# Differential attention: ScalarE copies turned weights ahead of the exponentials in every batch, the second rotary swap moves behind the first output, and unit 7's coefficients are made one batch sooner

## The reference

```python
q1, q2 = _rope(qb[:, :, 0], cos, sin), _rope(qb[:, :, 1], cos, sin)
k1, k2 = _rope(kb[:, :, 0], cos, sin), _rope(kb[:, :, 1], cos, sin)
p1 = jax.nn.softmax(jnp.where(mask, z1, -jnp.inf), axis=-1)     # z1 = q1 k1^T * scale, block of 128 queries
p2 = jax.nn.softmax(jnp.where(mask, z2, -jnp.inf), axis=-1)
w = p1 - lam * p2
out = w @ v
```

## Time and profile before

| what | value |
|---|---|
| median of 3 runs | 1461.81 us |
| profiled execution | 1462.43 us |
| its span | 1460.6 us |
| TensorE matmul busy | 1441.8 us (99%) |
| VectorE busy | 1010.9 us (69%) |
| ScalarE busy | 675.2 us (46%) |
| GpSimd busy | 356.9 us (24%) |
| granted TensorE clock | 0.998 of full |

### The profile page before, as it was taken

How to read it: one execution, slowest core, us unless ns; L and a number is a source line. 1 busy time by engine, 2 the same in 40 slices (tenths; PEclk the granted TensorE clock), 3 DMA queues, 4 the chain that set the end, 5 groups by cost and what they waited for, 6 DMA issues and landing times. The chain is left out here.

```text
span 1460.6 us, 19172 instructions
## 1 busy us (share of the span) xinstructions
PE 1441.8 (99%) x6960; PEld 1198.1 (82%) x6960; DVE 1010.9 (69%) x1293; ACT 675.2 (46%) x1092; POOL 356.9 (24%) x278
## 2 busy tenths in 40 slices
PE   9999999999999999999999999999999999999997
PEld 7888888887888888888888878888888888888886
DVE  6676876778868668574456788666664567678767
ACT  4454554546557667442122335444444434433343
POOL 4544454456444244212330220000000000000004
PEclk9999999999999999999999999999999999999999
DMA  5111112111111001013632334444444588836553
GB/s 198 44 39 49 58 44 72 57 58 59 44 46 42 30 15 43 30 58 101 211 106 83 114 99 163 179 146 144 154 158 154 206 276 295 293 131 200 190 198 132
DMA packets 76832, 172.38 MB, mean 118 GB/s; under 512 B 6097, under 2 KB 30929, under 8 KB 76625
## 3 DMA queue, kind: packets, MB, share of 16 engines
q1 hardware_dynamic: 76752, 171.33, 34.4%
HBM read 127.27 MB, written 44.04 MB: 117 GB/s over the span
## 5 line engine op out<-in xcount | busy, mean ns | idle before, releaser
L783 PE MATMUL p_proj<-xt_h,w_hi 128*128 128x512 f32 x616 | 244.3, 397 | 0.0
L787 PE MATMUL p_proj<-xt_h,w_lo 128*128 128x512 f32 x616 | 243.2, 395 | 0.0
L785 PE MATMUL p_proj<-xt_l,w_hi 128*128 128x512 f32 x616 | 241.7, 392 | 0.0
L2329 POOL TENSOR_TENSOR w_lo<-w_raw,w_hi 128x512 fp32r<-128x512 f32 x92 | 126.6, 1396 | 175.5 <-DVE w_hi L1630 174.9
L2452 POOL TENSOR_TENSOR row_odd<-row_odd,gains 128x1024 f32<-128x1024 f32 x4 | 10.4, 2622 | 579.1 <-ACT row_odd L1594 579.1
L787 PEld LDWEIGHTS p_proj<-xt_h,w_lo 128*128 128x128 f32 x616 | 115.8, 188 | 22.8
L783 PEld LDWEIGHTS p_proj<-xt_h,w_hi 128*128 128x128 f32 x616 | 115.9, 188 | 20.7
L785 PEld LDWEIGHTS p_proj<-xt_l,w_hi 128*128 128x128 f32 x616 | 115.9, 188 | 20.3
L1622 DVE TENSOR_TENSOR d_al<-f_a,d_ah 128x1024 fp32r<-128x1024 f32 x56 | 68.5, 1224 | 77.1 <-ACT d_ah L1511 77.0
L1511 ACT ACTIVATE d_ah<-f_a 128x1024 fp32r<-128x1024 f32 x56 | 59.3, 1058 | 131.4 <-PE p_av L1164 54.8
L1358 ACT ACTIVATE a_t<-p_tr 128x384 fp32r<-128x384 f32 (+3 forms) x96 | 47.3, 493 | 123.1 <-PE p_tr L872 122.7
(11 more groups left out here) (304 smaller groups left out, 3523.8 us busy)
## 6 DMA issues: line engine op xcount, KB each, us to landing
f_a<-h_terms SPq DMA_DIRECT2D x56, 512.0 KB, 3.4
h_terms<-c SPq DMA_DIRECT2D x40, 512.0 KB, 3.0
f_b<-w_ff SPq DMA_DIRECT2D x40, 512.0 KB, 4.8
w_raw<-w_in SPq DMA_DIRECT2D x39, 512.0 KB, 3.6
r<-w_ff SPq DMA_DIRECT2D x32, 512.0 KB, 3.8
gate_rows<-gst SPq DMA_DIRECT2D x12, 512.0 KB, 5.0
xt_raw<-xt SPq DMA_DIRECT2D x8, 512.0 KB, 8.2
wo_raw<-w_out SPq DMA_DIRECT2D x8, 512.0 KB, 8.7
```

What stands on the lines that cost most here:

```text
L783: pe.matmul(o, w_hi[n_slot][:, k, :], xt_h[:, k, cols], start=(k == 0), stop=False)
L785: pe.matmul(o, w_hi[n_slot][:, k, :], xt_l[:, k, cols], start=False, stop=False)
L787: mm = pe.matmul(o, w_lo[n_slot][:, k, :], xt_h[:, k, cols], start=False, stop=(k == KT - 1))
L2329: low = pool.tensor_tensor(w_lo[slot][:, ks, :], w_raw[:, ks, :], w_hi[slot][:, ks, :].bitcast(F32), ALU.subtract)
```

## The change

Four edits, in the differential groups alone:

1. ScalarE's copy of the turned weights (L1361) stands ahead of the exponentials in every batch. Before it did so in batches 2, 3, 7 and 8. Batch 0 and 1 have nothing to exchange, so it is batches 4, 5 and 6 that change.
2. The swap of half 1 of the first tile moves on ScalarE from right behind the copy of batch 1 to the end of that batch, behind the output of unit 0.
3. VectorE's `rope_half` of the same half moves from batch 0 to the end of batch 1, so behind the peaks of unit 3 and the cast of the next weight tile.
4. VectorE's `combine(7)` moves from batch 9 to batch 8, so ahead of the two `k_hi` casts.

```diff
     def later_halves(self, k):
 
-        if k in (2, 5):
+        if k in (0, 2, 5):
             return []
-        return self.halves_at(k - 1) if k in (3, 6) else self.halves_at(k)
+        return self.halves_at(k - 1) if k in (1, 3, 6) else self.halves_at(k)
...
-                    copy_first = not G.sb and (u, b) in ((2, 0), (3, 0), (5, 1), (6, 0))
+                    copy_first = not G.sb
                     while scored and not copy_first:
                         exponentials(*scored.pop(0))
                     act.wait_ge(tr_done, G.tr(k + 2) + 1)
...
                         act.activation(w_t[:, k % 2, 0:n * P], p_tr[:, 0:n * P], ACT.Copy).then_inc(tr_read, 1)
-                        if k == 1:
-                            project_done(G.halves_at(0))
                     while scored and copy_first:
                         exponentials(*scored.pop(0))
...
                     if G.sb:
                         project_done(G.halves_at(k))
-                    elif k:
+                    else:
                         project_done(G.later_halves(k))
...
-                        if (b == 0 if u == 5 else last_b) and 1 < u < G.nunits - 1:
+                        if (b == 0 if u in (5, 6) else last_b) and 1 < u < G.nunits - 1:
                             combine(u + 1)
```

## The result

The changed kernel is slower: 1463.88 us median of 22 runs (1463.30 to 1465.23) against 1461.74 us of before (22 runs, 1461.31 to 1462.07). The ratio is 1.0015, its 95% interval 1.0008 to 1.0021. The forecast was 1460.9 us, 0.9 us less than before, and its range ended at 1462.9: the time went the other way, by 2.1 us. That is 0.15%. It is clear of the noise, but it is under the 0.2% (2.9 us) that the prediction had called the line for a difference.

A forecast was written before the change was run, and what follows sets the result against it. TensorE, busy 99%, was taken as the bound, so only its stops could change. Gone 3.36 + 2.68 = 6.04 us, added 2.77 + 2.4 = 5.17 us, net 0.87 us less: 1460.9 us, range 1458.8 to 1462.9.

The forecast's parts named there:

- Part 1: Swap behind unit 0's output, rope_half a batch later: the excess from turn(2) to turn(3) goes, 3.36 us.
- third rival: Weight tile lands late, VectorE waits, the stop only moves from turn(2) to turn(3): 1464.3 us, chance 0.04.
- Part 2: combine(7) in batch 8: 2.68 us gone before turn(10), 2.4 us lost to later k_lo at three group transitions.
- the row from the kernel's start: Profile row of the same casts with k_lo taking 7.89 us, used to take a 0.8 us stop per transition.
- The rule's stop of 0.4 us: Alternative at the next group's first scores: by the port-lock rule k_lo takes 7.2 us, ending at 531.3.
- Part 3, batch 4: Copy ahead of exponentials: scores 12 start 1.96 us behind turn(4), in four groups, costing 2.77 us.
- Part 3, batch 6: Copy ahead of exponentials (6, 1): at most 0.6 us later, scores needing them about 3 us behind, no cost.
- The rivals: Alternative totals: 1458.5 or 1455.8 us (0.11 for the two), 1466.0 us (0.06), 1464.3 us (0.04).
- The slower one: At the group's end, the casts' whole shift passes to k_lo: TensorE stops 2.5 us three times, 1466.0 us, chance 0.06.

The follow-up runs named there:

- part1: The kernel before with only the swap moved behind unit 0's output and rope_half moved to the end of batch 1: 1457.93 us, ratio 0.9974.
- part12: The changed kernel with ScalarE's copies ahead of the exponentials only where they were before: 1457.51 us, ratio 0.9971.
- copy4: The kernel before with ScalarE's copy ahead of the exponentials in batch 4 too, nothing else: 1464.16 us, ratio 1.0019.
- no6: The changed kernel with the exponentials ahead of the copy again in batch 6 only: 1460.30 us, ratio 0.9992.
- no4: The changed kernel with the exponentials ahead of the copy again in batch 4 only: 1460.58 us, ratio 0.9994.
- copy6: The part12 kernel with the copy ahead of the exponentials in batch 6 too: 1460.85 us, ratio 0.9994.
- cast_late: The changed kernel with VectorE's weight tile cast moved from batch 6 to batch 7, behind the peaks (7, 1): 1463.70 us, ratio 1.0014.
- c7_late: The changed kernel with combine(7) back in batch 9, behind the k_hi casts: 1462.56 us, ratio 1.0005.
- split_cast: The part12 kernel with combine(7) between the two k_hi casts: 1457.39 us, ratio 0.9970.
- hold_swap: The changed kernel with two small 64 x 64 copies on ScalarE ahead of batch 6's swap: 1461.37 us, ratio 0.9998.

## Why the prediction was wrong

- **Part 1, 3.36 us gone: right.** turn(2) to turn(3) went from 6.04 to 4.93 us, and the edit alone gave 3.7 us (part1). The edit also shortened turn(3) to turn(4) by 0.07 to 0.09 us and turn(4) to turn(5) by 0.05 to 0.14 us a group, which covers the rest. VectorE did come early to the weight tile and waited for its transfer, 0.97 us in group 4 and 0.45 us in group 5 of the changed kernel, but turn(3) did not stop, so the third rival did not come:

```profile
495.76 0.87 DVE L1628 CAST w_hi<-w_raw 128x1024 fp32r<-128x1024 f32 x1 [0.45 <-DMA w_raw<-w_in]
```

- **Part 2, net 0.28 us gone (2.68 against 2.4): right in kind, and near in the net by some luck.** Measured 0.4 us (part12 against part1), since both terms were over-sized and the errors partly cancel. What goes at turn(10) is 2.3 us by start times, where I took 2.68. What comes at the first scores is 1.9 us, where I took 3 x 0.8 = 2.4: in group 5 of the changed kernel the first scores start 0.77 us behind the matmul before them, 0.55 us more than the 0.22 us of a row without a stop, and by the first turn of the next group 0.63 us are lost. The set of `k_lo` took 7.5 us, and not 7.89:

```profile
524.84 4.00 POOL L2353 TENSOR_TENSOR k_lo<-stage,k_hi 64x512 fp32r<-64x512 f32 x2 [3.26 <-DVE k_hi L1636]
529.00 3.32 POOL L2353 TENSOR_TENSOR k_lo<-stage,k_hi 64x512 fp32r<-64x512 f32 x2 [0.16 <-POOL k_lo L2353]
```

  By the rule of the Trainium skill (page "SBUF — State Buffer", section "SBUF: two separate sides") the estimate had been 7.2 us, the row from the kernel's start 7.89; the measured 529.00 + 3.32 - 524.84 = 7.48 us lies between them. I had named why the row might be long, a fourth piece beside another cast, and did not take it off. The rule's stop of 0.4 us is the idle time that the list shows (0.38 us), but not the 0.6 us that were lost.
- **Part 3, batch 4, 2.77 us added: right.** Scores 12 started 1.95 us behind turn(4), forecast 1.96. The edit alone cost 2.45 us (copy4). Batches 4 and 5 together cost 1460.30 - 1457.51 = 2.8 us (no6 against part12), so batch 5 cost little or nothing; no4, with the exchanges of batches 5 and 6, took 1460.58 us, and copy6, with that of batch 6 alone, 1460.85.
- **Part 3, batch 6, "No cost there": the step that failed.** It cost 3.3 us (copy6 against part12). It came as a stop at values(8) of 0.8 us in groups 4 to 6, from turn(8) to turn(10) 7.04 us in copy6's group 6 against 5.89 us in part12. I had followed the exponentials (6, 1) only as far as the scores that wait for them, and asked whether they come in time. I had not followed them to VectorE, where combine(6), the peaks (7, 0) and the weight tile's cast stand behind them in one queue, and had not asked what GpSimd does at that moment. Starts 0.3 us later were enough, since the cast had been only 0.11 us ahead of the sines. In group 7, without sines, the stop does not appear, though its ScalarE has the same order.
- **The rivals.** None was this one. The slower one had the right engine pair at the wrong place (the group's end), and cast_late shows it at smaller size: stops of 1.4 to 1.5 us where the rival had 2.5.

From the runs, 1461.7 - 3.7 - 0.4 + 2.8 + 3.3 = 1463.7 us, where 1463.88 was measured: the parts account for the result, and what the forecast missed is batch 6. The terms hold in this order of adding them; taken out of the changed kernel, the early combine(7) gives 1.3 us back (c7_late), because its gain before turn(10) is lost at values(8) already.

## What to carry to other kernels

When an instruction is moved by a few tenths of a microsecond, look at every pair of VectorE and GpSimd instructions behind it that start within that distance of each other: which of them starts first can be worth more than the move (here 0.3 us of delay, three times, cost 3.3 us). Follow a delayed result down each queue that holds it, and not only to the one that is known to be critical. In a bundle of edits test them apart: here two gave 4.2 us, and the exchange took 2.8 us in batch 4 and 3.3 us in batch 6.

## What the runs showed of the hardware

- A cast of 128x1024 and a GpSimd product of 128x512 that start 0.1 to 0.3 us apart hold each other up: 0.69 and 1.72 us when the cast is first (before, group 5), 1.57 and 1.29 us when it is second (changed kernel, group 5). From the first start to the last end it is 1.83 and 1.84 us, so the pair takes the same, and the order decides who pays: 0.43 us on the sines or 0.88 us on the cast.
- VectorE's large coefficient instruction (128x1024, two inputs in on-chip memory) took 1.29 us with GpSimd idle, 1.59 us beside `k_lo` in the kernel before, 1.93 us beside it in split_cast, and 2.40 us beside GpSimd's low part of a weight tile (cast_late), all in group 5 but the first, which is group 7's.
- Two 64x64 copies, 0.40 us of added ScalarE work, made the changed kernel 2.5 us faster by holding GpSimd's sines back by 0.26 us (hold_swap).
